# Quarter rows gathered over 128 partitions and turned by the vector engine, in a hybrid decoder step with a 32-expert mixture

## What is computed

```
x1 = layer_norm(ALPHA * x + mix @ w_out)
logits = x1 @ w_router + b_router;  top 4, softmax -> gate_w
for each expert e, for the tokens that chose it:
    h = clamped_swiglu(x1 @ w_gate[e] + b_gate[e], x1 @ w_up[e] + b_up[e])
    y = (h @ w_down[e] + b_down[e]) * gate_w
out[token] += y
x2 = layer_norm(ALPHA * x1 + out)
```

## Time and profile before

| what | us |
|---|---|
| median of 3 runs | 1417.76 (1416.95 to 1422.5) |
| the profiled execution, time | 1416.46 |
| the profiled execution, span of its instructions | 1414.6 |
| first phase, up to the first expert product | 336.5 |
| experts, up to the last product | 1045.4 |
| after the last product | 32.7 |

### The profile page before, as it was taken

The page is one execution under the profiler, slowest core; times in us unless marked ns, Lnnn a source line. Parts: engine busy times, 40 slices in busy tenths (PEclk is TensorE's granted clock), DMA queues, the critical chain, the costliest instruction groups (busy, mean ns, idle before and its releaser), DMA issues.

```text
span 1414.6 us, 43598 instructions
## 1 busy us (share of the span) xinstructions
PE 1358.3 (96%) x19522; PEld 872.2 (62%) x19522; DVE 440.2 (31%) x859; ACT 299.1 (21%) x637; POOL 120.4 (9%) x121
## 2 busy tenths in 40 slices
PE   7999999998999999999999999999999999999990
PEld 6767776555566666666666666666666666666660
DVE  3335656365322222222222222222222222222214
ACT  4544566131111111111111111111111111111104
POOL 1022000001010001000000100010000000100000
PEclk9999999998999999999999999999999999999995
DMA  8211042567999999999999999999999999999954
GB/s 276 60 50 46 16 145 74 210 234 280 413 405 397 405 401 405 397 403 403 406 403 403 403 403 396 403 401 407 397 404 401 408 401 401 401 399 389 405 216 135
DMA packets 78700, 459.80 MB, mean 325 GB/s; under 512 B 13344, under 2 KB 14896, under 8 KB 29232
## 3 DMA queue, kind: packets, MB, share of 16 engines
q1 hardware_dynamic: 67760, 429.74, 75.6%
q0 software_dynamic: 10256, 27.13, 7.2%
q10 hardware_dynamic: 512, 0.26, 0.1%
HBM read 443.85 MB, written 21.70 MB: 329 GB/s over the span
## 4 chain that ended last, share of the span: by engine, by line
PE 89%; DVE 6%; ACT 2%; issue 1%; DMA 1%; DVEq 0%; SPq 0%; ACTq 0%; POOLq 0%
PE unit L1274 47%; PE unit L1255 15%; PE unit L1258 9%; PE unit L1164 4%; PE unit L1243 3%; PE unit L763 2%; PE unit L765 2%; PE unit L764 2%; PE unit L758 1%; PE unit L891 1%; DVE attT L2185 1%; PE unit L915 1%; PE unit L798 1%; PE unit L1237 0%; ACT sbuf L1570 0%
## 5 line engine op out<-in xcount | busy, mean ns | idle before, releaser
L1274 PE MATMUL unit<-ring_b,xeT 128*32 128x256 f32 x6336 | 353.8, 381 | 1.1 <-ACT xeT L1420 1.1
L1274 PE MATMUL unit<-ring_a,xeT 128*32 128x256 f32 x5952 | 328.7, 379 | 0.0
L1274 PEld LDWEIGHTS unit<-ring_b,xeT 128*32 128x32 f32 x6336 | 203.7, 110 | 135.6 <-issue 2.7
L1274 PEld LDWEIGHTS unit<-ring_a,xeT 128*32 128x32 f32 x5952 | 192.6, 110 | 126.5
L1258 PE MATMUL unit<-ring_a,heT 128*32 128x256 f32 x768 | 169.7, 379 | 0.0
L1255 PE MATMUL unit<-ring_a,heT 128*32 128x512 f32 (+1 forms) x1536 | 169.4, 486 | 0.0
L1816 ACT ACTIVATE sg<-gm 128x768 f32<-128x768 f32 x32 | 27.0, 843 | 633.5 <-DVE gm L2456 633.5
L1258 PE MATMUL unit<-ring_b,heT 128*32 128x256 f32 x720 | 160.3, 379 | 0.0
L1255 PE MATMUL unit<-ring_b,heT 128*32 128x256 f32 (+1 forms) x1440 | 160.1, 486 | 0.0
L2484 DVE TENSOR_TENSOR hb<-unit,brow 128x768 f32<-128x768 f32 x32 | 30.7, 958 | 308.1 <-PE unit L1274 308.1
L700 POOL DMA_INDIRECT acc_rows<-ysb,idx x32 | 46.5, 1453 | 666.0 <-ACT ysb L1827 634.3
(11 more groups left out here) (318 smaller groups left out, 1264.8 us busy)
## 6 DMA issues: line engine op xcount, KB each, us to landing
ring_b<-w_gate_dram SPq DMA_DIRECT2D x68, 1024.0 KB
ring_a<-w_down_dram SPq DMA_DIRECT2D x68, 1024.0 KB
ring_b<-w_up_dram SPq DMA_DIRECT2D x64, 1024.0 KB
ring_a<-w_up_dram SPq DMA_DIRECT2D x64, 1024.0 KB
ring_a<-w_gate_dram SPq DMA_DIRECT2D x60, 1024.0 KB
ring_b<-w_down_dram SPq DMA_DIRECT2D x60, 1024.0 KB
raw_a<-w_in_dram SPq DMA_DIRECT2D x16, 512.0 KB, 3.7
wo<-w_out_dram SPq DMA_DIRECT2D x2, 1024.0 KB, 7.9
```

The lines of the kernel that those rows point to most:

```text
L1274: ins = mm(dst, stat(j), own[:, q], start=first and j != 1, stop=last and j != 0)
```

## The change

Three parts.

1. **Gather.** The DRAM table is now read as rows of quarters: each token has 4 quarters of 256 + 32 floats (1152 bytes), the gate weights repeated behind each. The columns are dealt so that a quarter holds every fourth block of 64. Slot s = 32 j + lane and quarter q go to partition 32 q + lane of part j, so gather(n) is three indirect DMAs (j = 0, 1, 2) of 128 numbers. `to_quarters` (one small PE product) and `quarter_rows` (two DVE operations) make these numbers from the old ones. `x_turned` (three DVE transposes in 32 x 32 blocks, 128 x 256 each) writes `xeT` straight from the gathered rows: `x_T` on PE and the copy of `px` on ACT are gone. From expert 4 on (`n >= TURN`) POOL waits for the landing of one of the three before it issues the next.
2. **Table.** POOL first copies each tile of `x1` into the new column order (`x1_by_quarter`), then writes it; gate weights are written four times each.
3. **Routing.** The transposes and the router product of tile 4 (samples) stand inside the last `out_product(3)`, behind its 5th and 6th step of 8, and `route(4)`, `gate(4)` stand on DVE ahead of `first_norm(3)`. Two stretches of filler products on PE before `logit4` are dropped.

The index work of an expert is done one expert earlier than before. A path for experts with over 96 tokens is adapted too.

```diff
             def gather(n):
-                at = idx[:CAP, n % TURN:n % TURN + 1]
-                pool.indirect_dma_start(xg[:CAP], None, x1_dram, bass.IndirectOffsetOnAxis(ap=at, axis=0),
-                                        bounds_check=T - 1, oob_is_err=False).then_inc(x_rows, 16)
+                for j in range(3):
+                    if j and not (isinstance(n, int) and n < TURN):
+                        pool.wait_ge(x_rows, n * 48 + 16 * j)
+                        pool.sem_inc(turn_over, 1)
+                    pool.indirect_dma_start(xq[:, j], None, x1_quarters,
+                                            bass.IndirectOffsetOnAxis(ap=idxq[:, j:j + 1], axis=0),
+                                            bounds_check=4 * T - 1, oob_is_err=False).then_inc(x_rows, 16)
+
+            def x1_by_quarter(n, i):
+                r = rows(i)
+                if n >= 2:
+                    pool.wait_ge(x1_out, 16 * n)
+                ps(nc.gpsimd.tensor_copy(x1q[n % 2][:r].rearrange("p (q c b) -> p c q b", q=4, c=4),
+                                         res[:r, i].rearrange("p (c q b) -> p c q b", c=4, q=4)))
+                ps.settle()
+                pool.dma_start(x1_dram[i * P:i * P + r].rearrange("t (q f) -> t q f", q=4)[:, :, 0:QUARTER],
+                               x1q[n % 2][:r].rearrange("p (q f) -> p q f", q=4)).then_inc(x1_out, 16)
...
             def pool_step(e, par, first=False):
                 if not isinstance(e, int) or e < NE - 2:
-                    pool.wait_ge(idx_ready, e + 3)
-                    pool.wait_ge(xT_done, e + 2)
+                    pool.wait_ge(idxq_ready, e + 3)
+                    pool.wait_ge(gcol_ready, e + 2)
                     pool.wait_ge(xe_ready, e + 2)
-                    pool.wait_ge(x_rows, (e + 2) * 16)
+                    pool.wait_ge(x_rows, (e + 2) * 48)
                     pool.sem_inc(turn_over, 1)
-                    gather(par + 2)
+                    gather(e + 2)
...
                     if m == 12:
                         sp.wait_ge(x1_ready, NT)
-                        sp.wait_ge(x_rows, 16)
+                        sp.wait_ge(x_rows, 48)
...
-            out_product(3)
+            def samples_routed(k):
+                if k == 4:
+                    x1_transposes(4)
+                if k == 5:
+                    logits(4)
+
+            out_product(3, samples_routed)
             x1_transposes(2)
-            x1_transposes(4)
             keep_running("logit2", 2)
             logits(2)
-            keep_running("logit4", 2)
-            logits(4)
...
-            def x_T():
-                for k in range(KD):
-                    half = xg[:CAP, k // 2 * 256:(k // 2 + 1) * 256].rearrange("s (p k) -> s k p", k=2)[:, k % 2]
-                    ins = tr(px[:, k * P:k * P + CAP], half, ident[:CAP, :CAP])
-                ins.then_inc(xT_done, 1)
+            def to_quarters(n, out):
+                pe.wait_ge(idx_ready, n + 1)
+                mm(out, laneb[:CAP], spread[:CAP].rearrange("p j c -> p (j c)"), start=True, stop=True)\
+                    .then_inc(spread_done, 1)
...
             def pe_step(e, p2, m0):
                 no_more = e >= NE - 2
-                pe.wait_ge(x_rows, (e + 2) * 16)
-                pe.wait_ge(xe_ready, e + 1)
-                x_T()
                 if not no_more:
-                    pe.wait_ge(picked, e + 3)
-                    pe.wait_ge(gate_read, e + 2)
-                    rows_of(tok_done, CAP)
+                    pe.wait_ge(idxq_ready, e + 2)
+                    to_quarters(e + 2, px[:, 0:9])
+                if e + 3 < NE:
+                    pe.wait_ge(picked, e + 4)
+                    pe.wait_ge(idx_ready, e + 3)
+                    rows_of(px, tok_done, CAP)
                 pe.wait_ge(h_ready, e + 1)
...
             def rows_in(n, par):
-                act.wait_ge(xT_done, n + 1)
...
-                copy(xeT[:, par], src).then_inc(xe_ready, 1)
+                act.wait_ge(x_rows, (n + 1) * 48)
+                for j in range(3):
+                    at = n + (j * QCOLS + QUARTER)
+                    own = slice(j * NS, (j + 1) * NS)
+                    src = xg[own, at:at + 1] if isinstance(n, int) else xg[own, bass.ds(at, 1)]
+                    ins = copy(gcol[own, par:par + 1], src)
+                ins.then_inc(gcol_ready, 1)
...
+            def quarter_rows(n, src):
+                v.wait_ge(spread_done, n + 1)
+                tt(row_parts[:, :, 0:3], ...
+                v.wait_ge(row_half, 2 * n + 2)
+                    red(idxq[:], row_parts[:], ALU.add).then_inc(idxq_ready, 1)
+
+            def x_turned(n, par):
+                v.wait_ge(x_rows, (n + 1) * 48)
+                v.sem_inc(turn_over, 1)
+                for j in range(3):
+                    src = xq[:, j, 0:QUARTER].rearrange("p (c a k) -> p c k a", c=4, k=2)
+                    ins = nc.vector.transpose(xeT[:, par, j], src)
+                ins.then_inc(xe_ready, 1)
...
             def dve_step(e, par):
...
                 over_partitions(1, e, up_bias_in)
                 if not no_more:
-                    v.wait_ge(y_free, e + 1)
-                    read_rows(e + 2, (par + 2) % TURN)
+                    quarter_rows(e + 2, px[:, 0:9])
...
                 turned(heT_last if last else heT, e)
+                if not (isinstance(e, int) and e >= NE - 3):
+                    v.wait_ge(y_free, e + 2)
+                    read_rows(e + 3, (par + 3) % TURN, px)
...
                     gate_sig(e + 1)
+                if not no_more:
+                    x_turned(e + 2, par % 2)
```

More of the change, by code:

```diff
@@ L46 @@
 MAXEXTRA = T * TOPK // (CAP + 1)
-XROWS = T + P
-XCOLS = D + NE
-KEEP = dict(ident=P, tokv=NT * 3, slot=4, jcol=MAXEXTRA)
+QUARTER = D // 4
+QCOLS = QUARTER + NE
+XCOLS = 4 * QCOLS
+KEEP = dict(ident=P, tokv=NT * 3, slot=4, jcol=MAXEXTRA, lane=P, third=9, quarter=12)
 EARLY = dict(cum=P, rest=P, cum_s=NS, rest_s=NS, before=P, ones=P, upto32=2 * NE, cos=NT * ROT, sin=NT * ROT,
@@ L151, in build @@
         ranks = sb("ranks", [P, ORDERS, P])
-        here[0] += (2 * (FOLD - QUARTER) - (ORDERS - 1) * P) * 4
+        laneb = sb("laneb", [P, P], BF16)
+        spread = sb("spread", [P, 3, 3], BF16)
+        row_parts = sb("row_parts", [P, 3, 4])
+        idxq = sb("idxq", [P, 3], I32)
+        here[0] += 1600
         raw_at = here[0]
@@ L299, in build @@
         here[0] = phase_at
-        xeT = sb("xeT", [P, 2, KD, CAP])
+        xeT = sb("xeT", [P, 2, 3, KD, NS])
         after_xeT = here[0]
@@ L1153, in mix_T, with out_product @@
                 transposes(f"mixT{i}", src, i)
-            def out_product(i):
+            def out_product(i, between=None):
                 name = f"out{i}"
@@ L1169, in out_product @@
                                      start=k == 0, stop=k == KD - 1)
+                    if between is not None and k < KD - 1:
+                        between(k)
                 ins.then_inc(s_full(name), 1)
@@ L1317, in _ @@
             pe.wait_ge(picked, 1)
-            rows_of(tok_done, CAP)
+            rows_of(pg, tok_done, CAP)
+            to_quarters(0, pg[:, 1008:1017])
             extra_offsets()
             gates_T()
-            pe.wait_ge(idx_ready, 1)
+            pe.wait_ge(idxq_ready, 1)
             pe.wait_ge(picked, 2)
-            rows_of(tok_done, CAP)
+            rows_of(pg, tok_done, CAP)
             down_bias(0, 1)
+            to_quarters(1, pg[:, 1008:1017])
             pe.wait_ge(freed[3], USES[3] + 1)
-            pe.wait_ge(x_rows, 16)
-            x_T()
+            pe.wait_ge(picked, 3)
+            rows_of(px, tok_done, CAP)
             pe.wait_ge(xe_ready, 1)
-            pe.wait_ge(idx_ready, 2)
+            pe.wait_ge(idxq_ready, 2)
             product(pg, x_of(0), 0, range(4))
@@ L1784, in _ @@
             gate_exp(2)
-            gate_exp(4)
             gate_exp(3)
@@ L2322, in gate @@
             def gate(i):
-                n, r = TILES.index(i), rows(i)
+                n, r = ROUTED.index(i), rows(i)
                 v.wait_ge(g_exp, n + 1)
@@ L2345, in _ @@
             gate(1)
+            route(4)
+            gate(4)
+            st(cp(row_part[:, 3:4], k_("slot")[:, 3:4]))
             first_norm(3)
             route(2)
-            route(4)
             gate(2)
-            st(cp(row_part[:, 3:4], k_("slot")[:, 3:4]))
             route(3)
-            gate(4)
             gate(3)
@@ L2373, in rows_of_slots, with read_rows @@
                     return red(out, row_part[:n], ALU.add)
-            def read_rows(n, col):
+            def read_rows(n, col, src):
                 v.wait_ge(tok_done, n + 1)
-                rows_of_slots(idx[:CAP, col:col + 1], CAP, (row_half, n + 1)).then_inc(idx_ready, 1)
-            v.wait_ge(ranks_in, 16)
+                with nc.allow_low_precision(reason="row numbers: whole and small"):
```

(31 more changed lines are left out.)

132 lines of the change are left out of this document (74 added, 58 removed).

## The result

The changed kernel takes 1394.55 us, median of 3 runs (1392.44 to 1396.08), against 1417.76: ratio 0.983, 95% interval 0.980 to 0.986. It is 23 us faster; the forecast was 1403.2.

What follows compares the result with a forecast made beforehand. PE and DMA were taken as both full. 1416.46 + 0.9 - 1.8 - 32.4 = 1383.2 us if PE alone counts, plus 20.0 for the waits between gather parts: 1403.2, range 1383 to 1428.

Steps and rivals of the forecast that it cites:

- 0.9 - 1.8 = -0.9: Start of the products: first product 0.9 us later, expert 0 1.8 us shorter without x_T and a wait.
- forecast of PE alone: Experts 1 to 30 without x_T: 32.4 us less, PE's period 31.46 instead of 32.55, total 1383.2.
- gather chain: Three gathers in a row, parts landing in 8.8 us, scatter to xeT 40.1: period 32.2, +20.0 us in 27 experts.
- (a): Rival, the forecast itself: waits between gather parts set the period, parts land in 8.5 to 9.1, 1392 to 1414 us; 45%.
- (b): Rival: PE's work alone sets the time, gather parts land in 8.3 us or less, 1383 us; 17%.
- DMA's load: Transfers an expert: need falls from 32.7 to 32.3 us, as quarters landing in all 128 partitions relieve the slower engine half.
- (c): Rival: the weights' stream sets the time because the gather disturbs it as before, 1410 to 1424 us; 22%.
- (d): Rival: slower, waits between gather parts that land in 9.6 us give period 33.6, 1441 us; 14%.
- copy to the table: POOL's copy of a tile before each table write: up to 2.4 us, hidden; if not, adds up to 2.
- chunks 12 to 15: Weight chunks issued after the first gather: they start 2.4 us later because its last part lands later.
- new order of routing: First phase, samples' routing moved into the last output product: net gain 0.5 us, between -2 and +1.
- signs that I had named: Profile: PE idle before gate some 0.7 us an expert, POOL idle from 20.7 to near nothing, over 367 GB/s around gathers.

Runs made afterwards that it cites:

- spaced_1: The changed kernel with one fill on POOL in place of each of the two waits between an expert's gathers; 1391.63 us, ratio 0.982.
- no_waits: The changed kernel without POOL's waits between the three gathers of an expert; 1428.98 us, ratio 1.006.
- light kernels: The kernel before (also with one of eight transposes) and the changed kernel, each without a third of the gate and up products; 1401.27 and 1384.21 us.
- light_96: The changed kernel without a third of the gate and up products, gathers from the fifth expert on held to 96 partitions; 1398.57 us.
- one_turn: The kernel before, old gather kept, with one of the eight transposes of each x_T; 1411.74 us, ratio 0.994.
- early_chunks: The changed kernel with weight chunks 12 and 13 issued without the wait for the first gather; 1393.31 us, ratio 0.982.

## Why the prediction was right in sign and 9 us too high

The products of the experts bound the sum, so it can be checked marker by marker, from the chain of both kernels. Between the starts of `up`, after against before:

- *Before `up(0)`: 353.27 against 351.26, +2.0.* The forecast said 0.9 - 1.8 = -0.9. Of the difference 3.1 were there before the new gather and routing can act: the last output product began 3.1 us later in this profile, most of it because products of the first phase ran at half the clock (granted 0.63 on average from 162 to 166 us and 0.72 from 220 to 226). Taken out, +4.4 at the first product is 1.3 (forecast 0.9), and expert 0 gave 2.4 (forecast 1.8).
- *From `up(0)` to `up(2)`: 68.03 us against 67.83, +0.2.* The forecast said 2.2 less. This is the stall again: gathers 2 and 3 belong to the written-out experts and have no waits, and the chain above shows it at 407.88. POOL's timeline there:

```profile
404.26 1.10 POOL L694 DMA_INDIRECT xg<-x_rows,idxq  x1 [9.29 <-issue]
405.67 1.01 POOL L694 DMA_INDIRECT xg<-x_rows,idxq  x1 [0.30 <-issue]
406.98 0.99 POOL L694 DMA_INDIRECT xg<-x_rows,idxq  x1 [0.30 <-issue]
```

  I had counted the missing waits as free. They cost 2.4 us in this profile (in spaced_1 and no_waits, where the first issue of gather 3 took 1.63 and 1.38, that gather brought one stall of 0.32); a version with the waits there too would be some 0.2% faster by this count. It wasn't tried.
- *From `up(2)` to `up(30)`: 27.3 us less; the forecast of PE alone said 30.3.* (`up(30)` starts at 1304.83, before at 1329.93.) Most of what lacks is the period: it is 31.55 and not 31.46, as the small products for the index numbers come to 0.11 instead of 0.06 and `rows_of` to 0.22 instead of 0.19 (the chain's rows at 831.16 and 831.27):

```profile
831.16 0.11 PE unit L1290
831.27 0.22 PE unit L1284 x5
```

- *From `up(30)` to the last product's end, 1358.28, before 1381.90: 53.45 against 51.97, +1.5,* the most of it PE's waits for weights. (The 3% of DMA in the chain is the transfer of one such chunk, 29.26 us long, and not what PE waited.) After the last product 32.3 us remain (forecast 32.7).

So PE alone would have given 1383.2 in the forecast, and came out at 1392.4.

**The step that failed is the gather chain, 20 us.** I took 8.8 us for the landing of a part, and so 10.0 from one issue to the next. From issue to issue it is 6.7 and 6.9 in the rows above; without waits (no_waits), a part lands in

```profile
DMA to landing us min/median/max: 5.5/6.2/7.6
```

where the old gather took 9.2. I had scaled only the bytes' share of the 9.2 and called the rest the queue of weights ahead of it. The rest was not fixed: a part of 128 numbers for rows of 1152 bytes lands 3 us sooner than one gather of 96 numbers for rows of 4224. Why is not shown. Nor has the third part only 16 valid numbers, as I wrote: by the way the slots are dealt (below) the three parts are filled about alike. The chain still has 7 us of room (38.6 - 31.3), so the mechanism of (a) never acted: the time came out as (b), PE alone, plus what the list above adds. That it lies in (a)'s 1392 to 1414 is luck: 20 us that were not there stood in for some 9 that I had not seen. Rival (b) said that parts of 8.3 or less give that case, which held. The estimate by the Trainium skill (DMA: Bandwidth & Descriptors, "Anatomy of one DMA") of 2.3 for a part had the right side; beside weights the trace has 6.2, and its number decides.

**DMA's load was right in size, for a wrong reason.** I gave the new kernel 32.3 us of transfers an expert and the old 32.7; the light kernels have 32.29 and 32.97. The packets are not four times as many either: the gathers' and scatters' queue has 11280 against 10256 by the two pages, 32 more an expert. But my reason, that the old rows land in partitions 0 to 67 and so load one half of the engines, is wrong. I had overlooked `slot_ranks`: it deals the slots over blocks of six partitions from 0 to 95, so that the rows are spread over all of these. What is told ahead of the prediction, that the rows fill the partitions from 0 up, has the same fault. The lag of half of the engines is there in both kernels. By the Trainium skill (DMA: Bandwidth & Descriptors, "The descriptor swizzle") a 128-partition transfer splits between eight engines for partitions 0 to 63 and eight for the others; that fits a lag of exactly half, but no run here ties the lag to the gathers' rows. That a gather on 96 partitions costs more than one on 128 is measured (light_96), its cause is open.

**The rivals.** (c), the weights' stream, is what the old gather does: forecast 1410 to 1424, and one_turn gave 1411.7, with a little less taken from PE than in the changed kernel. With the new gather it is near: transfers need 32.29 an expert and PE 31.55, so the lead of the ring shrinks by 0.74 in each, 22 us over 30 experts, and it is used up at the end, where the first waits for weights stand. In one_turn the same lead went at 32.97 - 31.68 = 1.3 an expert and was gone after some 20. (d) needed parts over 9.2 us and is out. A slower kernel did exist, by a mechanism that was in no list of mine: the same gathers without their waits.

**The small terms.** The copy to the table takes 1.04 (I bounded it by 2.4) and hides. The chunks 12 to 15 start 3.1 later by the change (forecast 2.4) and this costs nothing, as early_chunks shows. The new order of routing is worth 0.15 us in the trace (forecast 0.5) and nothing in the times. Of the signs that I had named, the idle of POOL between scatter and `y` did shrink, PE's wait for transposes did not appear, and the rate around a gather rose.

## What to carry to other kernels

Where PE and DMA are both full, what an edit takes from PE alone is largely given back by DMA: of some 26 us here 8 were left. Price the transfers with a kernel in which PE is made light, and compare the two needs before the edit. And a wait that looks like pure cost can keep issues apart; count what comes closer together when there is none.

## What was not expected of the hardware

- Three indirect gathers issued by GpSimd 0.30 us behind one another stop TensorE's weight loads in most experts two or three times for some 0.57 us each: 1.2 us an expert, some 33 us in all. Issued 1.3 us apart they don't, though all are in flight. It isn't the rows moved: with 16 of 128 partitions it is the same, and two of the stalls are over before a packet of the gathers moves.
- An indirect gather by 128 numbers of rows of 1152 bytes lands in 6.2 us beside a full stream of weights, one by 96 numbers of rows of 4224 bytes in 9.2 (8.8 in one_turn).
- Three gathers on 96 partitions cost the transfers 0.34 us more than three on 128 with a third more bytes, at an equal number of packets.
